# Eight slabs of each gated layer computed by seven block products instead of eight, in a two-block transformer kernel

## The chip, the cores and the metric
One core of one Trainium2 chip (trn2). The metric is the device time of one execution in microseconds; the kernel of before has a median of 1393.8 us over 3 runs (1392.55 to 1393.85).

## The reference, cut to what matters
The program computes two transformer blocks on 512 tokens of width 1024, in float32. Each ends in a gated feed-forward layer of width 2816 (22 tiles of 128). Only these two layers and the down projections behind them are touched:

```
# first block
h = h + (silu(hn @ w_gate) * (hn @ w_up)) @ w_down        # 1024 -> 2 x 2816 -> 1024
# second block: u = h @ w_up, a convolution of 3 taps over the tokens, then
# silu(u[:, :2816]) * u[:, 2816:], then @ w_down
```
Everything is computed to float32's precision. A float32 product on TensorE is made of three fp32r products, with each operand split in a high and a low part: hi x hi + hi x lo + lo x hi.

## The kernel before
**Data and slabs.** Activations lie feature-major, `[128, k, 512]`: feature within a tile of 128, tile k of 8, token. Weights are streamed from HBM as 111 slabs of 1 MB, `[128, 8, 256]`, in one order (`STREAM`): each holds 256 output columns for all 1024 inputs. In the gated layers slab t holds 128 columns of the gate and the 128 matching ones of the value, and its two results go to two banks of PSUM, a pair; `lin` has four banks, so two pairs. Slab g uses buffers `raw[g % 2]`, `whi[g % 2]`, `wlo[g % 2]`, and both layers start at an even g.

**A slab's way.** SyncE loads it into `raw` when GpSimd has finished with the slab two before (`wlo_ready`). ScalarE makes the high part `whi` in one instruction (L419, L746, L851), when TensorE has finished with the slab two before. GpSimd makes the low part `wlo = raw - whi` in four quarters (`low_quarter`, L392). TensorE waits for `wlo_ready` and for its pair of banks (`pair_free`) and issues for each of 2 x 8 tiles the three products of `three` (L1397 to L1401), 48 of 512 columns (`slab_fm`, L1403; `project`, L1439). In four slabs ("mix_tm") the roles are turned: the tokens are stationary and the weights move, 96 products of 256 columns each.

**The gated layers.** After each slab of the first layer VectorE multiplies both banks with the tokens' `rstd` (L1215, L1216) and frees the pair, makes one tile of the modulation that the second block needs (`ada_tile`, L1206; 48 tiles in all, the first 22 here), and multiplies gate and value (L1223). ScalarE makes the next high part first, then the silu (L748), then the high part of the product, `fh` (L750). VectorE makes the low part `fl` (L1225). In the second layer ScalarE evacuates both banks with scale and bias (L847), makes the next high part (L851), the silu (L853) and `fh` (L855); VectorE adds four shifted taps (L1362 to L1368), gates (L1372) and makes `fl` (L1375). Both layers are loops of 11 turns over two slabs. `fh` and `fl` take 44 KB per partition each, in an 88 KB region whose other tenants are dead by then.

**Down** (L1788) is 12 slabs: for each of 4 pairs of output tiles 8, 8 and 6 tiles of the 22 are contracted. Its first three slabs wait until as many low parts exist as they read (8, 16, 22). While it runs VectorE makes 18 more modulation tiles and the residual.

**Order.** Every engine's instructions are executed in the order in which they are written; only semaphores couple the engines. Large tensors start at multiples of 128 bytes (`rstd` is rounded to that, small tensors to 64, which puts `con` at 64 modulo 128).

## Time and profile before
| what | value |
|---|---|
| median of 3 runs | 1393.8 us |
| the profiled execution's own time | 1392.41 us |
| its span in the profile | 1390.6 us |
| instructions | 17280 |
| first gated layer, TensorE | about 481 to 720 us |
| second gated layer, TensorE | about 1025 to 1267 us |

A time in the profile counts from the start of the span. PE is TensorE's products, PEld its weight loads, DVE VectorE, ACT ScalarE, POOL GpSimd. "x4" after a row means that four instructions were merged, and its duration is that of all. A product's duration is longer than the distance to the next one, since products are pipelined; distances between starts give the pace.

### The profile page before, as it was taken

To read this page: it belongs to the slowest core of one execution; us is meant where nothing else is said; L and a number is where in the kernel's file an instruction comes from. 1 tells how busy PE (TensorE), PEld (TensorE's weight loads), DVE (VectorE), ACT (ScalarE), POOL (GpSimd) and SP (SyncE) were. 2 spreads that over 40 slices of the span, in tenths; PEclk is the share of its full clock that TensorE was granted. 3 is DMA by queue.
4 is the path that set the end of the run, shared out by engine and by line. 5 is a ranking of instruction groups with operands and counts; after the bars stand their busy time and mean duration, and the time that the engine had idled before them with its cause. 6 is when DMAs were issued, how large, how long until landed. Compare 5 with 4: busy or idle time off the path is not lost.

```text
span 1390.6 us, 17280 instructions
## 1 busy us (share of the span) xinstructions
PE 1358.4 (98%) x6530; PEld 1091.2 (78%) x6530; DVE 663.4 (48%) x978; ACT 623.4 (45%) x867; POOL 613.5 (44%) x448
## 2 busy tenths in 40 slices
PE   9999999999999999999999999988999999999999
PEld 7877955888876888888888887854878888888887
DVE  5434948355452553444343317588255455554111
ACT  5555228553364443444432123688244545554211
POOL 3444320474430455556554544312326555555453
PEclk9999999999999999999999999999999999999999
DMA  7223211152210244444446433200312222323422
GB/s 269 91 90 102 79 48 74 61 182 91 91 66 27 91 152 141 144 153 151 136 140 268 169 134 106 92 31 31 122 61 90 90 95 96 110 90 136 181 92 91
DMA packets 29215, 155.23 MB, mean 112 GB/s; under 512 B 3056, under 2 KB 4464, under 8 KB 14960
## 3 DMA queue, kind: packets, MB, share of 16 engines
q1 hardware_dynamic: 29168, 154.57, 31.2%
q8 instruction: 34, 0.56, 0.2%
q14 instruction: 13, 0.11, 0.0%
HBM read 152.46 MB, written 2.10 MB: 111 GB/s over the span
## 4 chain that ended last, share of the span: by engine, by line
issue 39%; PE 30%; POOL 26%; DVE 4%; DMA 1%; POOLq 0%; SPq 0%; ACT 0%
POOL wlo L392 26%; PE lin L1399 10%; PE lin L1401 10%; PE lin L1400 10%; DVE small L1044 1%; DVE expd L1055 1%; DMA raw<-w_slabs 1%; PE lin L1616 0%; DVE win L1276 0%; DVE small L1048 0%; POOLq L401 0%; DVE xl L923 0%; PE c_act L1455 0%; PE att L1470 0%; PE att L1464 0%
## 5 line engine op out<-in xcount | busy, mean ns | idle before, releaser
L392 POOL TENSOR_TENSOR wlo<-raw,whi 128x512 fp32r<-128x512 f32 x444 | 613.3, 1413 | 761.7 <-ACT whi L419 501.3
L1399 PE MATMUL lin<-xh,whi 128*128 128x512 f32 x1072 | 420.3, 392 | 4.1 <-POOL wlo L392 3.6
L1401 PE MATMUL lin<-xh,wlo 128*128 128x512 f32 x1072 | 417.3, 389 | 0.0
L1400 PE MATMUL lin<-xl,whi 128*128 128x512 f32 x1072 | 417.2, 389 | 0.0
L419 ACT ACTIVATE whi<-raw 128x2048 fp32r<-128x2048 f32 x66 | 126.6, 1919 | 260.3 <-PE lin L1401 254.9
L1399 PEld LDWEIGHTS lin<-xh,whi 128*128 128x128 f32 x1072 | 201.2, 188 | 52.4 <-issue 7.6
L1401 PEld LDWEIGHTS lin<-xh,wlo 128*128 128x128 f32 x1072 | 201.2, 188 | 42.1
L1400 PEld LDWEIGHTS lin<-xl,whi 128*128 128x128 f32 x1072 | 201.3, 188 | 41.6 <-issue 0.5
L1399 PE MATMUL lin<-fh,whi 128*128 128x512 f32 x352 | 137.0, 389 | 0.0
L1401 PE MATMUL lin<-fh,wlo 128*128 128x512 f32 x352 | 136.9, 389 | 0.0
L1400 PE MATMUL lin<-fl,whi 128*128 128x512 f32 x352 | 136.9, 389 | 0.0
L1206 DVE CUSTOM_DVE_ANT_0 adar<-adar,c_act 128x1024 f32<-128x1024 f32 x48 | 57.8, 1214 | 41.4 <-DMA adar<-ada 41.1
L1401 PEld LDWEIGHTS lin<-fh,wlo 128*128 128x128 f32 x352 | 66.1, 188 | 13.9
L1400 PEld LDWEIGHTS lin<-fl,whi 128*128 128x128 f32 x352 | 66.1, 188 | 13.8
L1399 PEld LDWEIGHTS lin<-fh,whi 128*128 128x128 f32 x352 | 66.1, 188 | 13.7 <-issue 0.3
L1138 DVE SCALAR_TENSOR_TENSOR h<-lin,mod,h 128x512 f32<-128x512 f32 x16 | 11.9, 750 | 118.5 <-PE lin L1401 118.5
L1362 DVE SCALAR_TENSOR_TENSOR tmp<-lin,convp,tmp 128x511 f32<-128x511 f32 x44 | 31.2, 750 | 68.3 <-ACT tmp L847 68.3
L746 ACT ACTIVATE whi<-raw 128x2048 fp32r<-128x2048 f32 x22 | 42.2, 1920 | 40.5 <-PE lin L1401 40.4
L1136 DVE TENSOR_TENSOR h<-lin,h 128x512 f32<-128x512 f32 x24 | 16.4, 691 | 84.2 <-PE lin L1401 84.1
L1215 DVE TENSOR_TENSOR tmp<-lin,rstd 128x512 f32<-128x512 f32 x22 | 15.2, 692 | 82.3 <-PE lin L1401 82.1
L1399 PE MATMUL lin<-xah,whi 128*128 128x512 f32 x128 | 50.7, 396 | 0.0
L1401 PE MATMUL lin<-xah,wlo 128*128 128x512 f32 x128 | 49.9, 390 | 0.0
(334 smaller groups left out, 1923.8 us busy)
## 6 DMA issues: line engine op xcount, KB each, us to landing
raw<-w_slabs SPq DMA_DIRECT2D x111, 1024.0 KB, 4.8
adar<-ada SPq DMA_DIRECT2D x48, 512.0 KB, 5.6
decay<-decay SPq DMA_DIRECT2D x4, 512.0 KB, 7.8
h<-x_t SPq DMA_DIRECT2D x3, 512.0 KB, 6.5
out_t<-h SPq DMA_DIRECT2D x3, 512.0 KB, 8.1
rope<-rope SPq DMA_DIRECT2D x2, 512.0 KB, 7.3
memx<-mem_t SPq DMA_DIRECT2D x1, 1024.0 KB, 5.7
adar<-c_row SPq DMA_DIRECT2D x2, 512.0 KB, 6.2
```

The source lines that it names most:

```text
L392: return nc.gpsimd.tensor_tensor(wlo[s][:, ks, :], raw[s][:, ks, :], f(whi[s][:, ks, :]), ALU.subtract)
L419: nc.scalar.activation(whi[g % 2][:, :, :], raw[g % 2][:, :, :], ACT.Copy).then_inc(whi_ready, 1)
L746: nc.scalar.activation(whi[s][:, :, :], raw[s][:, :, :], ACT.Copy).then_inc(whi_ready, 1)
L1044: last = nc.vector.tensor_reduce(ring(j, "max")[:, e:e + 1], att[n % 4][:, 0:width(j)], AX.X, ALU.max, negate=True)
L1055: nc.vector.tensor_scalar(row, row, ring(j - 1, "inverse")[:, e:e + 1], None, ALU.mult).then_inc(a["norm"], 1)
L1136: ins = nc.vector.tensor_tensor(h[:, k, :], b[:, :], h[:, k, :], ALU.add)
L1206: return nc.vector.tensor_tensor_reduce(adar[s][:, :], adar[s][:, :], c_act[:, :], 1.0, 0.0, ALU.mult, ALU.add, total).then_inc(ada["acc"], 1)
L1215: nc.vector.tensor_tensor(tmp[s][:, :], lin[2 * p][:, :], rstd[:, :], ALU.mult).then_inc(ffn["g"], 1)
L1362: nc.vector.scalar_tensor_tensor(t[:, 1:T], b[:, 0:T - 1], convp[s][:, 4 * j:4 * j + 1], t[:, 1:T], ALU.mult, ALU.add).then_inc(ffn2["tap" ...
L1399: nc.tensor.matmul(out, whi_, xhi_, start=first, stop=False)
L1400: nc.tensor.matmul(out, whi_, xlo_, start=False, stop=False)
L1401: return nc.tensor.matmul(out, wlo_, xhi_, start=False, stop=last)
```

## The change
Slabs 5, 7, ... 19 (`SEVENS`) of each gated layer are computed in another way. The 1024 inputs are taken as even and odd tiles (two blocks of 4 tiles), the 256 columns of the slab as gate and value, the 512 tokens as two halves of 256. So the slab's product is one of 2 x 2 block matrices, which the exact scheme of Strassen and Winograd gives with seven block products and fifteen block sums. The sums:
- of the moving operand (activations), four `[128, 4, 256]` sums, once for each layer: `moving_sums` on VectorE, 3, 2, 2 and 2 instructions, two before slab 0's evacuation and one each after slabs 0 and 1; their high parts by ScalarE (`MOVING_HI`), their low parts `tl` by VectorE after slabs 2 and 3 (`moving_low`), both in the 88 KB region.
- of the stationary operand (weights), four `[128, 4, 128]` sums for each slab on VectorE, `weight_sums`.
- of the products: a copy of the first by ScalarE (`seven_copy`) and seven instructions of 256 columns on VectorE, `combine`, in `lin` and two further banks, `att[0:2]`.

TensorE issues for each of the seven phases 4 x 3 products of 256 columns. The seven stationary units are split one by one, high part by ScalarE and low part by GpSimd, 512 elements each. They take the place of `whi[1]` and `wlo[1]` and the upper part of the region; `raw[1]` is read directly. In each product one operand lies at 64 modulo 128 bytes and the other at 0: the sums of the activations, a11, a12 and s4 at 64, the plain activations, s1, s2, s3 and a22 at 0.

As the region is thus taken, the gated product is kept whole (`gated`), and is split only when slab 19 is through: parts 0 to 4 after slab 20, 5 to 21 after slab 21 on ScalarE. VectorE makes low parts 0 to 4 after slab 20; in the first layer 5 to 9 after slab 21 and 10 to 21 ahead of the modulation tiles, in the second 5 to 21 after slab 21. Down reads these. The loops of ScalarE, VectorE and TensorE over both layers are unrolled; the copies of the convolution's parameters (L1356) and of the modulation sum (L1220) are gone. In the second layer ScalarE's order for each slab is: the seven splits where slab t + 2 is a seven slab, the evacuation of slab t, the copy for slab t + 1, otherwise the plain high part, the silu. VectorE's there: `seven_ended`, four taps, combinations 1 and 2 of slab t + 1, the gating, combinations 3 and 4.

```diff
+SEVENS = range(5, 20, 2)
+LAST_SEVEN = SEVENS[-1]
+PHASES = ("a11", "s2", "s1", "s3", "a12", "s4", "a22")
+MADE = ("a11", "a12", "s1", "s3", "s2", "a22", "s4")
+GATED = {"ffn": 0, "ffn2": 1}
+MOVING_HI = {0: (0, 1), 1: (2,), 2: (3,)}
+GATED_HIGH = {20: range(0, 5), 21: range(5, FT)}
...
-        at[0] = -(-at[0] // 128) * 128
+        at[0] += (P - at[0]) % (2 * P)
...
+        gated = rg_sb("gated", [P, FT, T], 0)
+        gated_lo = rg_sb("gated_lo", [P, FT, T], 0, F32R)
+        gated_hi = rg_sb("gated_hi", [P, FT, T], 44, F32R)
+        sevens = region + 44 * 1024 + 64
+        th = sb("th", [P, 4, TT, COLS], F32R, offset=sevens)
+        tl = sb("tl", [P, 4, TT, COLS], F32R, offset=sevens + 16 * 1024)
+        t_sum = sb("t_sum", [P, 4, TT, COLS], offset=sevens + 16 * 1024)
...
+        for i, u in enumerate(("s1", "s2", "s3", "a22")):
+            unit_hi[u], unit_lo[u] = (sb(f"{u}_{n}", [P, TT, P], F32R, offset=w + 8192 + 2048 * i)
+                                      for n, w in (("hi", whi_at), ("lo", wlo_at)))
+        for i, u in enumerate(("a11", "a12", "s4")):
+            unit_hi[u], unit_lo[u] = (sb(f"{u}_{n}", [P, TT, P], F32R, offset=sevens + (32 + 6 * j + 2 * i) * 1024)
+                                      for j, n in enumerate(("hi", "lo")))
+        for u in ("s1", "s2", "s3"):
+            unit_sum[u] = sb(f"{u}_sum", [P, TT, P], offset=wlo_at + 8192 + 2048 * (int(u[1]) - 1))
+        unit_sum["s4"] = sb("s4_sum", [P, TT, P], offset=sevens + 42 * 1024)
...
+                    made = 0
+                    for u in MADE:
+                        if u == "s4":
+                            pool_e.wait_ge(whi_ready, g + 1)
+                        else:
+                            made += 1
+                            pool_e.wait_ge(seven["hi"], c["hi"] + made)
+                        if u in ("s1", "s2"):
+                            pool_e.wait_ge(seven["sum"], c["sum"] + (2 if u == "s1" else 4))
+                        full = PLAIN[u] if u in PLAIN else unit_sum[u][:, :, :]
+                        ins = nc.gpsimd.tensor_tensor(unit_lo[u][:, :, :], full, f(unit_hi[u][:, :, :]), ALU.subtract)
+                        if u == "a22":
+                            ins.then_inc(wlo_ready, 1)
+                        else:
+                            ins.then_inc(seven["lo"], 1)
...
+            def seven_hi(name, t):
+                g, n = SLAB0[name] + t, SEVENS.index(t)
+                c, before = seven_at(name, n), seven_at(name, n - 1)
+                act.wait_ge(raw_in[1], 16 * (g // 2 + 1))
+                for u in MADE:
+                    if u in PLAIN:
+                        if n and u != "a22":
+                            act.wait_ge(seven["mm"], before["mm"] + PHASES.index(u) + 1)
+                        else:
+                            act.wait_ge(slab_done, g - 1)
+                    else:
+                        act.wait_ge(seven["sum"], c["sum"] + int(u[1]))
+                    full = PLAIN[u] if u in PLAIN else unit_sum[u][:, :, :]
+                    ins = nc.scalar.activation(unit_hi[u][:, :, :], full, ACT.Copy)
+                    if u == "s4":
+                        ins.then_inc(whi_ready, 1)
+                    else:
+                        ins.then_inc(seven["hi"], 1)
+            def seven_copy(name, t, dst):
+                c = seven_at(name, SEVENS.index(t))
+                act.wait_ge(glu["y"], GATED[name] * FT + t - 1)
+                act.wait_ge(seven["mm"], c["mm"] + 1)
+                nc.scalar.activation(dst[:, 0:COLS], lin[2 * ((PAIR0[name] + t) % 2)][:, 0:COLS], ACT.Copy
+                                     ).then_inc(seven["copy"], 1)
...
+            def gated_high(name, t):
+                act.wait_ge(slab_done, SLAB0[name] + LAST_SEVEN + 1)
+                act.wait_ge(glu["y"], GATED[name] * FT + t + 1)
+                nc.scalar.activation(gated_hi[:, t, :], gated[:, t, :], ACT.Copy).then_inc(glu["hi"], 1)
...
+            for t in range(FT):
+                s, g = t % 2, SLAB0["ffn"] + t
+                if t + 2 in SEVENS:
+                    seven_hi("ffn", t + 2)
+                else:
+                    act.wait_ge(slab_done, g + 1)
+                    make_hi(g + 2)
+                if t + 1 in SEVENS:
+                    seven_copy("ffn", t + 1, tmp[1])
+                act.wait_ge(glu["first"], t + 1)
+                nc.scalar.activation(tmp[s][:, :], tmp[s][:, :], ACT.Silu).then_inc(glu["act"], 1)
+                for j in MOVING_HI.get(t, ()):
+                    moving_hi("ffn", j)
+                for j in GATED_HIGH.get(t, ()):
+                    gated_high("ffn", j)
...
+            def weight_sums(name, t, which):
+                n = SEVENS.index(t)
+                c, before, g = seven_at(name, n), seven_at(name, n - 1), SLAB0[name] + t
+                s1, s2, s3, s4 = (unit_sum[f"s{i}"][:, :, :] for i in range(1, 5))
+                ops = {1: (s1, A21, A22, ALU.add), 2: (s2, s1, A11, ALU.subtract), 3: (s3, A21, A11, ALU.subtract),
+                       4: (s4, A12, s2, ALU.subtract)}
+                for i in which:
+                    if i == 1:
+                        dve.wait_ge(raw_in[1], 16 * (g // 2 + 1))
+                    if n:
+                        dve.wait_ge(seven["mm"], before["mm"] + PHASES.index(f"s{i}") + 1)
+                    else:
+                        dve.wait_ge(slab_done, g - 1)
+                    if i in (2, 4):
+                        dve.wait_ge(seven["sum"], c["sum"] + i - 1)
+                    dst, a, b, op = ops[i]
+                    nc.vector.tensor_tensor(dst, a, b, op).then_inc(seven["sum"], 1)
...
+            def combine(name, t, which, s1):
+                c, p = seven_at(name, SEVENS.index(t)), 2 * ((PAIR0[name] + t) % 2)
+                low, high = slice(0, COLS), slice(COLS, T)
+                (ba, bd), (bb, bc) = lin[p:p + 2], att[0:2]
+                u2, u4 = tmp[3][:, low], tmp[3][:, high]
+                for i in which:
+                    if i == 1:
+                        dve.wait_ge(seven["copy"], c["copy"] + 1)
+                        dve.wait_ge(seven["mm"], c["mm"] + 2)
+                        ins = nc.vector.tensor_tensor(u2, bb[:, low], s1[:, low], ALU.add)
+                    if i == 2:
+                        dve.wait_ge(seven["mm"], c["mm"] + 3)
+                        dve.wait_ge(seven["add"], c["add"] + 1)
+                        ins = nc.vector.tensor_tensor(u4, u2, bd[:, low], ALU.subtract)
+                    if i in (3, 4):
+                        dve.wait_ge(seven["mm"], c["mm"] + 4)
+                        dve.wait_ge(seven["add"], c["add"] + 2)
+                        ins = nc.vector.tensor_tensor(bd[:, high] if i == 3 else u2, bc[:, low], u4 if i == 3 else u2, ALU.add)
+                    if i == 5:
+                        dve.wait_ge(seven["mm"], c["mm"] + 5)
+                        ins = nc.vector.tensor_tensor(ba[:, low], ba[:, high], s1[:, low], ALU.add)
+                    if i == 6:
+                        dve.wait_ge(seven["mm"], c["mm"] + 6)
+                        dve.wait_ge(seven["add"], c["add"] + 5)
+                        ins = nc.vector.tensor_tensor(ba[:, high], bb[:, high], u4, ALU.add)
+                    if i == 7:
+                        dve.wait_ge(slab_done, SLAB0[name] + t + 1)
+                        ins = nc.vector.tensor_tensor(bd[:, low], bc[:, high], u2, ALU.add)
+                    ins.then_inc(seven["add"], 1)
...
+            def seven_ended(name, t, s1):
+                if t + 2 in SEVENS:
+                    weight_sums(name, t + 2, (1, 2, 3))
+                combine(name, t, (5, 6), s1)
+                if t + 2 in SEVENS:
+                    weight_sums(name, t + 2, (4,))
+                combine(name, t, (7,), s1)
+                dve.wait_ge(seven["add"], seven_at(name, SEVENS.index(t))["add"] + 7)
...
+            for j in range(2):
+                moving_sums("ffn", norms["ffn"], j)
+            for t in range(FT):
+                s, p = t % 2, (PAIR0["ffn"] + t) % 2
+                if t in SEVENS:
+                    seven_ended("ffn", t, tmp[1])
+                dve.wait_ge(slab_done, SLAB0["ffn"] + t + 1)
+                nc.vector.tensor_tensor(tmp[s][:, :], lin[2 * p][:, :], rstd[:, :], ALU.mult).then_inc(glu["first"], 1)
+                nc.vector.tensor_tensor(tmp[2 + s][:, :], lin[2 * p + 1][:, :], rstd[:, :], ALU.mult).then_inc(pair_free, 1)
+                dve.wait_ge(ada_in[s], 16 * (t // 2 + 1))
+                ada_tile(s, mod[:, t:t + 1])
+                if t + 1 in SEVENS:
+                    combine("ffn", t + 1, (1, 2), tmp[1])
+                if t + 2 == SEVENS[0]:
+                    weight_sums("ffn", t + 2, (1, 2, 3, 4))
+                dve.wait_ge(glu["act"], t + 1)
+                dve.wait_ge(pair_free, PAIR0["ffn"] + t + 3)
+                nc.vector.tensor_tensor(gated[:, t, :], tmp[s][:, :], tmp[2 + s][:, :], ALU.mult).then_inc(glu["y"], 1)
+                if t + 1 in SEVENS:
+                    combine("ffn", t + 1, (3, 4), tmp[1])
+                if t < 2:
+                    moving_sums("ffn", norms["ffn"], t + 2)
+                elif t < 4:
+                    for j in (2 * t - 4, 2 * t - 3):
+                        moving_low("ffn", j)
+                for j in GATED_HIGH[20] if t == 20 else range(5, 10) if t == 21 else ():
+                    gated_low("ffn", j)
...
+                for j in range(10 + 6 * batch, 16 + 6 * batch):
+                    gated_low("ffn", j)
+            lows_beside_down(0)
+            lows_beside_down(1)
...
+                for j in GATED_HIGH[20] if t == 20 else range(5, FT) if t == 21 else ():
+                    gated_low("ffn2", j)
...
+                operands = dict(a11=(ba, plain(0, 0)), s2=(bb, summed(1)), s1=(bd, summed(0)), s3=(bc, summed(2)),
+                                a12=(ba, plain(1, 0)), s4=(bb, plain(1, 1)), a22=(bc, summed(3)))
+                for i, u in enumerate(PHASES):
+                    if i == 0:
+                        pe.wait_ge(pair_free, p + 1)
+                    if n == 0 and i == 1:
+                        pe.wait_ge(seven["add"], c["add"])
+                    if u == "a22":
+                        pe.wait_ge(wlo_ready, g + 1)
+                    else:
+                        pe.wait_ge(seven["lo"], c["lo"] + [m for m in MADE if m != "a22"].index(u) + 1)
+                    if u == "a12":
+                        pe.wait_ge(seven["copy"], c["copy"] + 1)
+                    if u == "s4":
+                        pe.wait_ge(seven["add"], c["add"] + 1)
+                    if u == "a22":
+                        pe.wait_ge(seven["add"], c["add"] + 4)
+                    bank, x = operands[u]
+                    e = int(u in ("a12", "s4", "a22"))
+                    for k in range(TT):
+                        mm = three(bank[:, COLS * e:COLS * (e + 1)], unit_hi[u][:, k, :], unit_lo[u][:, k, :], x[k][0], x[k][1],
+                                   k == 0, k == TT - 1)
+                    if u == "a22":
+                        mm.then_inc(slab_done, 1)
+                    else:
+                        mm.then_inc(seven["mm"], 1)
...
-                            pe.wait_ge(parts["lo"], ks[-1] + 1)
+                            pe.wait_ge(glu["lo"], base + ks[-1] + 1)
```

## Rows read from the trace of the kernel before

**Rows 1.** the page, part 1: busy time, share of the span, instructions of each engine
```profile
PE 1358.4 (98%) x6530; PEld 1091.2 (78%) x6530; DVE 663.4 (48%) x978; ACT 623.4 (45%) x867; POOL 613.5 (44%) x448
```

**Rows 2.** windows view, two slabs of the first gated layer, per engine
```profile
core 0: us, PE busy (x) PEld busy (x) DVE busy (x) ACT busy (x) POOL busy (x), PEclk, DMA share, GB/s
604.00:625.80 21.80, 21.80 (x98) 18.05 (x97) 8.86 (x14) 8.86 (x9) 11.92 (x9) 1.00 0.42 144
```

**Rows 3.** timeline of TensorE in the first gated layer: start, duration, instruction
```profile
520.20 0.39 PE L1399 MATMUL lin<-xh,whi 128*128 128x512 f32 x1
...
522.92 0.39 PE L1399 MATMUL lin<-xh,whi 128*128 128x512 f32 x1
```

**Rows 4.** timeline of TensorE in the token-major projections
```profile
149.90 0.28 PE L1399 MATMUL lin<-whi,xh 128*128 128x256 f32 x1
...
152.90 0.28 PE L1400 MATMUL lin<-wlo,xh 128*128 128x256 f32 x1
```

**Rows 5.** timeline of TensorE at the start of the first down projection
```profile
719.89 0.39 PE L1401 MATMUL lin<-xh,wlo 128*128 128x512 f32 x1
720.12 0.39 PE L1399 MATMUL lin<-fh,whi 128*128 128x512 f32 x1
```

**Rows 6.** timeline of GpSimd in the first down projection
```profile
744.13 5.02 POOL L392 TENSOR_TENSOR wlo<-raw,whi 128x512 fp32r<-128x512 f32 x4 [5.84 <-ACT whi L419]
```

**Rows 7.** timelines of VectorE, ScalarE and GpSimd, one slab of the first gated layer
```profile
611.52 0.69 DVE L1215 TENSOR_TENSOR tmp<-lin,rstd 128x512 f32<-128x512 f32 x1 [2.73 <-PE lin L1401]
612.73 1.21 DVE L1206 CUSTOM_DVE_ANT_0 adar<-adar,c_act 128x1024 f32<-128x1024 f32 x1
...
614.20 1.16 DVE L1223 TENSOR_TENSOR tmp<-tmp,tmp 128x512 f32<-128x512 f32 x1
616.38 0.69 DVE L1225 TENSOR_TENSOR fl<-tmp,fh 128x512 f32 x1 [1.02 <-ACT fh L750]
...
613.34 0.61 ACT L748 ACTIVATE tmp<-tmp 128x512 f32<-128x512 f32 x1
...
613.52 5.95 POOL L392 TENSOR_TENSOR wlo<-raw,whi 128x512 fp32r<-128x512 f32 x4 [3.58 <-ACT whi L746]
```

**Rows 8.** instructions grouped by line and form
```profile
L976 DVE TENSOR_TENSOR tmp<-tmp,rope 128x512 f32<-128x512 f32 x8 | 5.4, 681 | 0.0
L930 DVE TENSOR_TENSOR wlo<-raw,whi 128x512 fp32r<-128x512 f32 x3 | 2.0, 683 | 0.0
L1034 DVE TENSOR_TENSOR weight<-att,decay 128x256 f32<-128x256 f32 x8 | 3.0, 411 | 0.0
L1512 PE MATMUL att<-squares,con 128*128 128x512 f32 x8 | 3.8, 592 | 0.0
```

**Rows 9.** timeline of VectorE at the end of the residual before the first gated layer
```profile
483.88 1.77 DVE L881 TENSOR_TENSOR rstd<-rstd,tmp 128x512 f32<-128x512 f32 x1
```

**Rows 10.** timelines of ScalarE, VectorE and GpSimd, one slab of the second gated layer
```profile
1201.77 1.45 ACT L847 ACTIVATE tmp<-lin,convp 128x512 f32<-128x512 f32 x2 [2.42 <-PE lin L1401]
1203.11 1.91 ACT L851 ACTIVATE whi<-raw 128x2048 fp32r<-128x2048 f32 x1
...
1203.92 0.74 DVE L1365 SCALAR_TENSOR_TENSOR tmp<-lin,convp,tmp 128x511 f32<-128x511 f32 x1
...
1205.10 5.93 POOL L392 TENSOR_TENSOR wlo<-raw,whi 128x512 fp32r<-128x512 f32 x4 [3.67 <-ACT whi L851]
```

**Rows 11.** timeline of VectorE, first two slabs of the first gated layer
```profile
493.39 0.69 DVE L1215 TENSOR_TENSOR tmp<-lin,rstd 128x512 f32<-128x512 f32 x1 [0.23 <-DVE rstd L1202]
...
502.72 0.69 DVE L1215 TENSOR_TENSOR tmp<-lin,rstd 128x512 f32<-128x512 f32 x1 [2.72 <-PE lin L1401]
```

**Rows 12.** windows view around the softmax of the cross attention, columns as in rows 2
```profile
411.30:414.70 3.40, 2.43 (x14) 1.75 (x15) 3.33 (x7) 1.87 (x7) 3.40 (x3) 1.00 0.00 0
414.76:418.16 3.40, 3.40 (x6) 1.33 (x5) 0.91 (x4) 3.25 (x6) 0.24 (x1) 0.50 0.56 164
```

**Rows 13.** timeline of TensorE, f32 products from squares and con
```profile
127.20 1.88 PE L1512 MATMUL att<-squares,con 128*128 128x512 f32 x4
```

232 lines of the change are left out of this document (141 added, 91 removed).

## The prediction, made before the changed kernel ran
> **What bounds the kernel now.** The page comes first. TensorE is busy 98% of the span, VectorE, ScalarE and GpSimd under half [rows 1]. The windows view of one pair of slabs in the first gated layer shows the same: TensorE without a gap, the others busy for 9 to 12 of 21.8 us [rows 2]. So time is won only by giving TensorE less to do, and is lost wherever it is made to wait. The timeline then gives its pace. Twelve products of 512 columns take 520.20 to 522.92, 226.7 ns each [rows 3]; 25 products of 256 columns take 149.90 to 152.90, 120.0 ns each [rows 4]. Columns at 2.4 GHz are 213.3 and 106.7 ns, so about 13.3 ns per product come on top at either width. The boundary from the first gated layer to its down projection is also seamless: the next product starts 0.23 us after the last [rows 5].
>
> **1. TensorE's own work.** A plain slab is 48 products of 512 columns: 48 x 0.2267 = 10.88 us. A seven-product slab is 7 x 4 x 3 = 84 products of 256: 84 x 0.120 = 10.08 us. Arithmetic falls by an eighth, but there are more products, each with its 13.3 ns, so only 0.80 us is won. Sixteen slabs: **-12.8 us**. This is the whole gain; everything else can only take from it.
> The Trainium skill (TensorE: Matmul & The Clock Gate, Back-to-back issue gap) puts the fixed part of a warm product at 2.5 ns. By it the slabs would take 10.36 and 9.17 us and the gain would be 19.0 us. No fp32r row here shows so small a part, so the sum doesn't use it.
>
> **2. The price of a shared access.** The weights' low parts (GpSimd) meet VectorE instructions with two SBUF sources. GpSimd's four quarters take 5.02 us undisturbed [rows 6], 1.26 each, and 5.95 in a gated slab, where VectorE runs two such instructions [rows 7]: 0.46 more each. On VectorE's side one of 512 elements takes 0.68 alone [rows 8], but 1.77 when it must let a quarter finish [rows 9]. Side by side they thus alternate at 1.26 + 0.46 = 1.72 us a turn. The changed kernel adds such instructions: weight sums, moving sums and their low parts, and it moves the gated low parts together.
> The Trainium skill (SBUF — State Buffer, two separate sides) states the rule behind this and it speaks against the change: VectorE with two SBUF inputs and GpSimd lock each other out for a whole instruction. The trace agrees in kind; an entire lockout would add 0.68 rather than 0.46.
>
> **3. Steady state, per pair (even slab, seven slab, 20.96 us).** GpSimd: 4 quarters and 7 unit subtractions of the same 512 elements, 11 x 1.26 + 6 crossings x 0.46 = 16.6 us. ScalarE in the second layer, its fuller one: 1.92 for the plain weights, 7 x 0.61, a copy near 0.4, 4 x 0.73, 2 x 0.61: 10.7. VectorE there: 8 taps of 0.74, 2 gatings and 4 weight sums of 0.68 to 1.72, 7 combinations of 0.41 [rows 8]: 12.9 to 19.1. All fit. The order matters at one place: the low parts of the even slab that follows a seven slab. Count from the end of the even slab before. First layer: ScalarE's high part at once, 1.92; GpSimd 5.02 with one or two crossings, ready at 7.5; needed at 10.08. No wait. Second layer: ScalarE first evacuates the pair, 1.45 [rows 10], then the new copy, 0.4, then 1.92: 3.8. GpSimd needs 5.02 and crosses the gating and two or three weight sums for the slab after, 1.4: ready at 10.2 to 10.9, wanted at 10.08. Seven slabs wait about 0.35 us: **+2.5** (bounds 0 and 7 x 0.9 = 6). The products of the seven slab wait for nothing: first copy at 2.3 for the fifth product at 5.8, combinations 3 and 4 at 6.7 for the seventh at 8.6.
>
> **4. The front of each layer.** Before the first slab's evacuation VectorE makes the first two moving sums, 5 chained instructions of 1024 elements, 1.22 us each going by 411 and 683 ns for 256 and 512 [rows 8], 2.3 if GpSimd alternates. In the first layer they stand behind the reciprocal: first evacuation at 493.4 + 6.1 = 499.5 to 504, where it was 493.39; TensorE needs its banks when slab 1 ends, 502.7 [rows 11]. I take 1 us (0 to 2.5). In the second layer nothing is in the way. At slab 3 VectorE has, besides the evacuation, four weight sums, a gating that waits until ScalarE has split all seven units, and two moving lows of 1024; slab 5's second product waits for these at 12.3 us, and they end at 10 to 16. I take 1.5 and 1. Together **+3.5** (0 to 9).
>
> **5. The boundary to down.** Before, the gated high and low parts were made slab by slab, and down started with all but the last. Now their place is occupied by the seven scheme until slab 19, ScalarE makes parts 0 to 4 after slab 20 and 5 to 21 only after the silu of slab 21. Down's first slab waits for low parts 0 to 7. So parts 5 to 7 are entirely behind the end of slab 21. First layer, VectorE: two evacuations 1.37, modulation tile 1.29, gating 0.68, three lows 2.04: 5.4 us at least (ScalarE: 1.92 + 0.61 + 3 x 0.63, then a low, 5.1). GpSimd is subtracting the next weights from 2.0 on, so gating and lows alternate with its four quarters: 3.3 + 0.65, then three turns of 1.72: 9.2. Second layer: the evacuation costs 3.7, ScalarE reaches the silu at 4.05 behind 1.45 + 1.92, then gating and three lows: 6.8 at least, 10.7 alternating from 3.5. Rows of one such instruction after another beside GpSimd are nearest to alternation [rows 9], so I take 9.2 + 10.7: **+19.9** (12.2 to 19.9). Nothing covers this: TensorE has no other work there, and all later work shifts with it.
>
> **6. The clock.** Before 414.7 TensorE worked 2.43 of 3.40 us; in the 3.40 us that follow its clock is at half, 1.2 GHz [rows 12]. A pause of 9 us should do no less. Each such stretch costs up to 1.7 us if work falls in it: **+2.5** for two (0 to 3.4).
>
> **7. Without effect.** Unrolling removes ScalarE's table loads in the loops, and VectorE's convp copies and ada_sum copies go. They stood beside TensorE's work, which had no gap there, so they are worth nothing by themselves. SyncE's loads keep their conditions: the weights of an odd slab are requested once unit a22 of the odd slab before has been subtracted, about 4 us before that slab starts on TensorE, and their first new reader, ScalarE's first unit, comes 3 us after its start. In down the modulation tiles start after twelve more lows, but the weights' own condition comes later still. Moving rstd and tmp by 256 bytes keeps their position modulo 128.
>
> **Sum.** -12.8 + 2.5 + 3.5 + 19.9 + 2.5 = **+15.6 us**. The profiled execution took 1392.4 (span 1390.6), giving 1408.0; the median, 1393.8, is 1.4 higher, so 1409. All lower bounds: -12.8 + 12.2 = -0.6, or 1393; all upper: +25.5, or 1419.
>
> **Rivals.** (a) *Placement, faster.* Every fp32r operand of before lies at 0 modulo 128 bytes; in the changed kernel each small product has one operand at 0 and one at 64. The f32 products that have con at 64 show almost nothing on top: four take 1.88 us where one takes 0.59 [rows 8, 13], so 0.43 apart for two passes of 0.213. If the fixed part falls from 13.3 to 3 ns for these 1344 products, that is another -13.8. The even slabs of the second layer would then wait 0.85 longer (+6), so with the boundary at 19.9 the result stays slower, 1401. It turns below 1391 only where VectorE also wins the access at once (12.2, front and clock near 0): 1393.8 - 26.6 + 12.2 + 6 = 1385. Against: f32 products with both operands at 0 look no different. Chance of faster 0.12. (b) *No contention at the boundary.* VectorE gets in between the quarters each time, pauses of 5.4 and 6.8, the clock hardly falls: -0.6 to +2, 1393 to 1396. The single low part in rows 7 takes only 0.69 beside GpSimd, but it comes after a pause of VectorE. Chance 0.10. (c) *GpSimd becomes the bound.* It is at 16.6 of 21; if its unit subtractions over strided weights cost 2 us rather than 1.45, every odd slab starts late, 16 x 0.8 more: 1422. The same size takes 1.49 where VectorE crosses it [rows 7]; chance 0.08, inside slower. (d) *Boundary hidden*, gain 12.8 whole, 1381: excluded by the program order on ScalarE, except by a misreading; it is in the 0.12.
>
> **How the numbers follow.** My case and its neighbours between +3 and +25 hold 0.70, (c) 0.08, (b) 0.10, faster 0.12. A measurement of this kernel tells about 0.2% from nothing, 2.8 us. The range leaves out most of faster and part of (c): 1392 to 1419.
>
> **What would show it.** Starts of the 256-column products 120 ns apart confirm step 1; 109 would be rival (a). TensorE idle behind GpSimd's wlo before even slabs of the second layer only: step 3. One gap of about 9 and one near 11 us before down's first products, released by VectorE's gated_lo: step 5; under 7 both, rival (b). The granted clock at half right after each: step 6. A total under 1391 would prove the sum wrong.

## The result, and the profile after

| what | before | after |
|---|---|---|
| median, us | 1393.17 (4 runs, 1392.32 to 1393.85) | 1409.85 (4 runs, 1406.78 to 1411.55) |
| profiled execution, us | 1392.41 | 1409.14 |
| its span, us | 1390.6 | 1407.4 |

The change makes the kernel slower: ratio 1.0118, 95% interval 1.0098 to 1.0137. Of the page of after, busy time, share and instructions of each engine; these answer to [rows 1]:

```profile
PE 1346.3 (96%) x7106; PEld 1107.5 (79%) x7106; DVE 808.3 (57%) x1136; ACT 611.5 (43%) x945; POOL 695.4 (49%) x496
```
TensorE is busy for 12.1 us less and the span is 16.8 us longer: the work did shrink, and 28.9 us of idle TensorE came in.

**Where TensorE waits.** The timeline of TensorE in after, in order of time: before slab 2 of the first layer, at the boundary to down (answers to [rows 5]), before slab 5's second block product and before an even slab of the second layer, and at the second boundary:

```profile
503.75 0.39 PE L1638 MATMUL lin<-xh,wlo 128*128 128x512 f32 x1
506.26 0.47 PE L1636 MATMUL lin<-xh,whi 128*128 128x512 f32 x1 [2.12 <-DVE tmp L1432]
...
717.34 0.39 PE L1638 MATMUL lin<-xh,wlo 128*128 128x512 f32 x1
726.82 0.76 PE L1636 MATMUL lin<-gated_hi,whi 128*128 128x512 f32 x1 [9.09 <-DVE gated_lo L1409]
...
1092.19 0.39 PE L1636 MATMUL att<-th,s_hi 128*128 128x256 f32 x1 [1.55 <-DVE tl L1352]
...
1122.09 0.50 PE L1636 MATMUL lin<-xh,whi 128*128 128x512 f32 x1 [0.48 <-POOL wlo L430]
...
1271.48 0.39 PE L1638 MATMUL lin<-xh,wlo 128*128 128x512 f32 x1
1282.23 0.76 PE L1636 MATMUL lin<-gated_hi,whi 128*128 128x512 f32 x1 [10.36 <-DVE gated_lo L1409]
```
The bracket is the idle time and what ended it. Measured by starts (717.34 to 726.82 is 9.48, less the pace of 0.227), the two big pauses are 9.25 and 10.52 us and end with VectorE's last gated low part.

**Why VectorE is late there.** Timelines of VectorE and of GpSimd in after, from the end of the first layer's last slab:

```profile
717.76 0.69 DVE L1431 TENSOR_TENSOR tmp<-lin,rstd 128x512 f32<-128x512 f32 x1 [0.65 <-PE lin L1638]
...
718.97 1.21 DVE L1324 CUSTOM_DVE_ANT_0 adar<-adar,c_act 128x1024 f32<-128x1024 f32 x1
...
720.31 1.34 DVE L1441 TENSOR_TENSOR gated<-tmp,tmp 128x512 f32<-128x512 f32 x1
721.58 7.50 DVE L1409 TENSOR_TENSOR gated_lo<-gated,gated_hi 128x512 fp32r<-128x512 f32 x7
...
719.83 6.29 POOL L430 TENSOR_TENSOR wlo<-raw,whi 128x512 fp32r<-128x512 f32 x4 [4.48 <-ACT whi L488]
```
The gating takes 1.34 instead of 0.68, and seven low parts 7.50, while GpSimd's four quarters take 6.29 instead of 5.02 [rows 6]. TensorE resumes at 726.8, when GpSimd has just ended at 726.1.

**The clock.** Windows view of after, around the first boundary, columns as in [rows 2]:

```profile
705.00:717.70 12.70, 12.70 (x57) 10.20 (x55) 10.10 (x10) 5.04 (x7) 6.39 (x4) 1.00 0.41 137
...
719.80:730.00 10.20, 3.18 (x8) 2.54 (x9) 10.08 (x12) 10.18 (x19) 6.29 (x4) 0.50 0.41 140
```
Some 2.2 us into the pause the granted clock falls to a half, 1.2 GHz, for 10.24 us; the first eight products of down run in that stretch. At the second boundary the fall comes 4.4 us into the pause and lasts as long.

**The pace of the small products.** Timeline of TensorE in after, the starts of the seven block products of slab 11 in the order of `PHASES` (a11, s2, s1, s3, a12, s4, a22), and of the slab behind it:

```profile
624.07 0.28 PE L1636 MATMUL lin<-xh,a_hi 128*128 128x256 f32 x1
...
625.49 0.28 PE L1636 MATMUL att<-th,s_hi 128*128 128x256 f32 x1
...
626.90 0.28 PE L1636 MATMUL lin<-th,s_hi 128*128 128x256 f32 x1
...
628.32 0.28 PE L1636 MATMUL att<-th,s_hi 128*128 128x256 f32 x1
...
629.73 0.28 PE L1636 MATMUL lin<-xh,a_hi 128*128 128x256 f32 x1
...
631.10 0.28 PE L1636 MATMUL att<-xh,s_hi 128*128 128x256 f32 x1
...
632.46 0.28 PE L1636 MATMUL att<-th,a_hi 128*128 128x256 f32 x1
...
633.82 0.39 PE L1636 MATMUL lin<-xh,whi 128*128 128x512 f32 x1
```
Twelve products each: the first four take 1.41 to 1.42 us (117.5 to 118 ns a product), the last three 1.36 or 1.37 (113.3 to 114.2). The whole slab of 84 takes 9.75 us, 116.1 ns a product, and so do the others but slab 5 once their waits are taken off; that is neither the 120.0 of [rows 4] nor rival (a)'s 109.

### The profile page after: what moved, and what is told of

Its sections match the earlier page's. It is cut to its first block, busy times and chain, and to the rows that moved or that the text cites. A ratio compares the mean times of both kernels' runs of the same rounds, so it can differ in the third digit from the quotient of the medians.

```text
span 1407.4 us, 18385 instructions
## 1 busy us (share of the span) xinstructions
PE 1346.3 (96%) x7106; PEld 1107.5 (79%) x7106; DVE 808.3 (57%) x1136; ACT 611.5 (43%) x945; POOL 695.4 (49%) x496
## 4 chain that ended last, share of the span: by engine, by line
PE 47%; issue 24%; POOL 18%; DVE 8%; ACT 2%; DMA 0%; SPq 0%; POOLq 0%; DVEq 0%; ACTq 0%
POOL wlo L430 17%; PE lin L1636 14%; PE lin L1638 13%; PE lin L1637 13%; DVE small L1162 1%; PE att L1636 1%; DVE expd L1173 1%; PE att L1638 1%; PE att L1637 1%; ACT whi L488 1%; PE lin L2049 1%; DVE s_sum L1373 1%; ACT tmp L963 1%; DVE tl L1352 0%; DMA raw<-w_slabs 0%
## 5 line engine op out<-in xcount | busy, mean ns | idle before, releaser
L430 POOL TENSOR_TENSOR wlo<-raw,whi 128x512 fp32r<-128x512 f32 x380 | 526.9, 1418 | 691.8 <-ACT whi L488 660.7
L1636 PE MATMUL lin<-xh,whi 128*128 128x512 f32 x816 | 320.8, 393 | 9.9 <-POOL wlo L430 6.4
L1637 PE MATMUL lin<-xl,whi 128*128 128x512 f32 x816 | 317.8, 389 | 0.0
L1638 PE MATMUL lin<-xh,wlo 128*128 128x512 f32 x816 | 317.7, 389 | 0.0
L1636 PE MATMUL lin<-gated_hi,whi 128*128 128x512 f32 x352 | 138.7, 394 | 19.4 <-DVE gated_lo L1409 19.4
L1637 PE MATMUL lin<-gated_lo,whi 128*128 128x512 f32 x352 | 138.2, 393 | 0.0
L1638 PE MATMUL lin<-gated_hi,wlo 128*128 128x512 f32 x352 | 138.1, 392 | 0.0
L1636 PEld LDWEIGHTS lin<-gated_hi,whi 128*128 128x128 f32 x352 | 67.0, 190 | 34.1 <-issue 20.2
L466 POOL TENSOR_TENSOR s_lo<-s_sum,s_hi 128x512 fp32r<-128x512 f32 x64 | 91.8, 1455 | 1.5 <-DVE s_sum L1373 1.5
L466 POOL TENSOR_TENSOR a_lo<-raw,a_hi 128x512 fp32r<-128x512 f32 x48 | 79.0, 1660 | 3.3 <-ACT a_hi L513 3.3
```

The lines of the kernel that those rows point to most:

```text
L430: return nc.gpsimd.tensor_tensor(wlo[s][:, ks, :], raw[s][:, ks, :], f(whi[s][:, ks, :]), ALU.subtract)
L466: ins = nc.gpsimd.tensor_tensor(unit_lo[u][:, :, :], full, f(unit_hi[u][:, :, :]), ALU.subtract)
L1636: nc.tensor.matmul(out, whi_, xhi_, start=first, stop=False)
L1637: nc.tensor.matmul(out, whi_, xlo_, start=False, stop=False)
L1638: return nc.tensor.matmul(out, wlo_, xhi_, start=False, stop=last)
```

## The experiments

The twelve kernels fall in four groups, each timed beside the kernel before on the same chip. Code is cut at `...`. The kernel before had medians of 1393.75, 1392.42, 1391.9 and 1393.77 there, so a difference of a us or two across groups means nothing.

**First group (before 1393.75).** *1. The deferral alone.* All slabs plain, no sums, but the gated product is split as late as in the change and the loops stay unrolled.

```diff
-SEVENS = range(5, 20, 2)
-LAST_SEVEN = SEVENS[-1]
+SEVENS = ()
+LAST_SEVEN = 19
...
```


> The changed kernel with no seven-product slab at all: every slab plain, but the gated parts still split only after slabs 20 and 21, and the loops still unrolled. Theory (the boundary waits are the cost, and they come from the deferral alone): TensorE waits 9 and 10.5 us before the two down projections, about 3.7 us of half clock after them, no waits inside the layers, some 1.8 us gained in the second layer by the unrolling; 1393.2 + 9.1 + 10.4 + 3.7 - 1.8 = 1415 us. Rival (the seven-product machinery, its sums and its contention, is the cost): about the time of the kernel before, 1391 to 1396.

1414.10 us, ratio 1.0143 (1.0127 to 1.0158). The waits view of this kernel, TensorE (us in total, times, longest):

```profile
PE lin L1616 <- DVE gated_lo L1405: 19.5, 2, 10.4
```
All of the loss is the deferral. The seven products with everything they drag along are worth only about 4 us (1414.10 - 1409.85). In the second layer, moreover, TensorE has no pause at all between slabs, which bears on the unrolling below.

*2. All operands at 0 modulo 128 bytes.*

```diff
-        sevens = region + 44 * 1024 + 64
+        sevens = region + 44 * 1024 + 128
```


> The changed kernel with its new operands at 0 modulo 128 bytes instead of 64; the operations are the same. In the changed kernel's trace the products of the seven slabs start 113 to 118 ns apart, against 120 in the token-major projections. Theory (the distance comes from the two operands' places): they go back to 120 ns, 1344 x 2.7 ns = 3.6 us more, 1413.5. Rival (it comes from something else in these products, the placing does nothing): 117 ns and 1409.9 as before.

1413.28 us, ratio 1.0145 (1.0131 to 1.0159). Its timeline at the same block products:

```profile
628.09 0.28 PE L1636 MATMUL att<-th,s_hi 128*128 128x256 f32 x1
...
629.53 0.28 PE L1636 MATMUL lin<-xh,a_hi 128*128 128x256 f32 x1
...
630.96 0.28 PE L1636 MATMUL att<-xh,s_hi 128*128 128x256 f32 x1
```
1.44 and 1.43 us for twelve, 120.0 and 119.2 ns; a whole slab takes 10.03 us (119.4 ns a product) instead of 9.75. The placing is worth 16 x 0.28 = 4.5 us, of which 6 x 0.25 = 1.5 are given back, since the even slabs of the second layer wait 0.64 with it and 0.39 without. The medians are 3.4 us apart.

*3. Eight parts early.* ScalarE and VectorE split parts 0 to 7 after slab 20, all that down's first slab reads.

```diff
-GATED_HIGH = {20: range(0, 5), 21: range(5, FT)}
+GATED_HIGH = {20: range(0, 8), 21: range(8, FT)}
...
```


> The changed kernel with gated parts 0 to 7, not 0 to 4, split after slab 20, so that down's first slab waits for nothing that follows slab 21. Theory: the waits of 9.1 and 10.4 us shrink to about 2 and 3.5 us, in which VectorE ends the low parts, and the half clock after them mostly goes: 1409.9 - 14 - 3.5 = 1392. Rival (the wait only moves to down's second slab, which needs parts up to 15): the two waits reappear before it and the time stays over 1402.

1393.15 us, ratio 1.0003 (0.9992 to 1.0014). The two waits shrink from 19.8 to 1.49 + 2.76 us, and instead of two half-clock stretches of 10.24 at the boundaries there is one of 3.4. They didn't reappear in down's second slab.

*4. No GpSimd beside the low parts.* Parts 5 to 7 stay late, but after slab 21 ScalarE makes them ahead of the next weights' high part, so that GpSimd has nothing to subtract meanwhile.

```diff
-                else:
+                elif t < 21:
...
+                    if t == 21 and j == 8:
+                        make_hi(g + 2)
...
```


> The changed kernel with one change of order on ScalarE after slab 21 of each layer: silu and gated high parts 5 to 7 first, the high part of down's second slab of weights after them. GpSimd is then idle while VectorE makes low parts 5 to 7. Theory (VectorE's low parts lose 1 us each to GpSimd's quarters): TensorE's waits fall from 9.1 to about 5.5 and from 10.4 to about 7, 1402.5. Rival (VectorE is paced by ScalarE's high parts or its own work, not by GpSimd): the waits change by under 1 us each, 1409.

1403.83 us, ratio 1.0078 (1.0063 to 1.0094). Timelines of VectorE and GpSimd of this kernel at the boundary:

```profile
719.03 0.69 DVE L1445 TENSOR_TENSOR gated<-tmp,tmp 128x512 f32<-128x512 f32 x1
719.64 1.89 DVE L1413 TENSOR_TENSOR gated_lo<-gated,gated_hi 128x512 fp32r<-128x512 f32 x3
721.96 3.04 DVE L1413 TENSOR_TENSOR gated_lo<-gated,gated_hi 128x512 fp32r<-128x512 f32 x2 [0.44 <-ACT gated_hi L536]
...
721.48 4.68 POOL L430 TENSOR_TENSOR wlo<-raw,whi 128x512 fp32r<-128x512 f32 x3 [7.20 <-ACT whi L488]
```
The gating takes 0.69 and three low parts 1.89, and the moment GpSimd starts at 721.48 two low parts take 3.04. The pauses are 5.18 and 6.50, against 9.25 and 10.52: 4.1 and 4.0 us less. Some 0.2 of each come from an earlier silu and gating, the rest, 3.8 us a boundary, is what the shared access costs: 0.65 in the gating and 3.1 in the three low parts. That is the alternation of step 2, seen with and without its partner. The time fell by only 6 us, since the clock gave nothing back: its half-clock stretches are shorter (3.4 and 6.8 us) but lie wholly or mostly in down's work, whose first slab takes 12.6 and 13.5 us here, 12.5 and 12.9 in after and 10.88 in before.

**Second group (before 1392.42).** *5. The front.* In the first layer two moving sums each after slabs 0 and 1 and none before slab 0's evacuation; in both layers the low parts 2 and 3 ahead of slab 3's gating.

```diff
-            for j in range(2):
-                moving_sums("ffn", norms["ffn"], j)
...
-                    moving_sums("ffn", norms["ffn"], t + 2)
+                    for j in (2 * t, 2 * t + 1):
+                        moving_sums("ffn", norms["ffn"], j)
...
+                if t == 3:
+                    for j in (2, 3):
+                        moving_low("ffn2", j)
...
```


> The changed kernel with VectorE's sums placed otherwise: in the first layer the moving sums 0 and 1 after slab 0's evacuation and gating, 2 and 3 after slab 1's; in both layers the moving lows 2 and 3 ahead of slab 3's gating, which waits for ScalarE. Theory (the waits of 2.3 us before slab 2 of the first layer and of 2.35 and 1.7 us inside slab 5 of each layer are VectorE's order alone): all three go or fall under 0.5 us, 1409.9 - 6 = 1404. Rival (VectorE simply has too much to do by slab 5, wherever it stands): the wait before slab 2 goes, those inside slab 5 stay or grow, 1407 to 1409.

1403.97 us, ratio 1.0079 (1.0064 to 1.0095). Both waits of the first layer are gone, that of the second fell from 1.72 to 1.10 with 0.84 at the next even slab, and the boundary is untouched (9.27 and 10.53). The waits that went come to 2.3 + 2.4 + 0.6 - 0.8 = 4.4 us; the medians differ by 5.9, beside each kernel's own before by 5.1.

*6. Everything at once, with the order of test 4.* All eight seven slabs; eight parts early; TensorE waits tile by tile in down; the next slab's high part behind the gated ones to part 11; the copy behind the plain high part; the front of test 5.

> The changed kernel, still with eight seven-product slabs in each layer, with four mends together: gated parts 0 to 7 split after slab 20 and down waiting tile by tile instead of for eight at once; the high part of down's second slab of weights after gated high part 11; the sums placed as in the run on the front; in the second layer the copy of the first product after the plain high part. Theory (the waits are separate and additive, nothing else bounds): no wait over 0.5 us in either layer or at the boundaries, so 1393.2 - 1.8 (unrolling) - 16 x 1.0 = about 1376 to 1379. Rival (contention on VectorE and GpSimd brings new waits in their place): over 1385.

1387.52 us, ratio 0.9957 (0.9943 to 0.9970): faster than before, but far from the expected. Timelines of ScalarE, GpSimd and TensorE of this kernel in down's first slabs:

```profile
716.09 1.90 ACT L488 ACTIVATE whi<-raw 128x2048 fp32r<-128x2048 f32 x1
717.90 5.30 ACT L536 ACTIVATE gated_hi<-gated 128x512 fp32r<-128x512 f32 x10
...
718.07 6.36 POOL L430 TENSOR_TENSOR wlo<-raw,whi 128x512 fp32r<-128x512 f32 x4 [8.79 <-ACT whi L488]
...
724.49 0.50 PE L1644 MATMUL lin<-gated_hi,whi 128*128 128x512 f32 x1 [1.96 <-POOL wlo L430]
```
The trick that helped in test 4 hurts here. The weights' high part, 4.3 us later behind slab 21 than in test 11 (5.7 in the second layer), is now what down's second slab waits for: 2.12 us here and 4.72 at 1266.6, with a half-clock stretch of 6.8 us around its end.

*7. Seven seven-slabs instead of eight.* Slab 19 becomes plain, so the region comes free two slabs earlier and the gated parts are spread over slabs 18 to 21. The copy, the tile-wise wait and the front as in test 6, the high part in its natural place.

```diff
-SEVENS = range(5, 20, 2)
+SEVENS = range(5, 18, 2)
...
-GATED_HIGH = {20: range(0, 5), 21: range(5, FT)}
+GATED_HIGH = {18: range(0, 4), 19: range(4, 9), 20: range(9, 15), 21: range(15, FT)}
...
```


> As the run before it in the list, but with seven-product slabs 5 to 17 only, seven in each layer, and the gated parts split during slabs 18 to 21, so that all but the last seven are ready when down begins. Theory: 14 x 1.0 + 1.8 us less than the kernel before and no waits, 1377 to 1380, about the same as with eight and mended boundaries. Rival (with 22 parts to split in four slabs VectorE is late): waits over 1 us before down, over 1382.

1380.12 us, ratio 0.9901 (0.9886 to 0.9916). Both boundaries are without a wait.

*8. The kernel before with its split weights 64 bytes further on.* If 64 modulo 128 helps small products, it might help all. The parameters and constants that lie behind the weights move along.

```diff
+        at[0] += 64
         whi = [sb(f"whi{i}", [P, KT, COLS], F32R) for i in range(2)]
```


> The kernel before, with one line: the weights' high and low parts (whi, wlo) start 64 bytes later, so that every slab product has its weights at 64 modulo 128 bytes and its activations at 0. No operation changes. Theory (two operands of an fp32r product at the same place modulo 128 bytes cost about 3 ns a product, as the run with aligned operands showed for the small ones): the distance of 512-column products falls from 226.7 to about 223, over 4000 products, 12 to 16 us, 1379. Rival (the effect is of the 256-column products alone, or of th and tl): 1393 to 1394.

1419.97 us, ratio 1.0188 (1.0170 to 1.0205): the opposite. The timeline of TensorE of this kernel, products of 512 columns:

```profile
619.76 0.39 PE L1400 MATMUL lin<-xh,whi 128*128 128x512 f32 x1
...
622.56 0.39 PE L1400 MATMUL lin<-xh,whi 128*128 128x512 f32 x1
```
Twelve products in 2.80 us, 233.3 ns each, where [rows 3] has 226.7. Those of 256 columns went the other way, from 120.0 to 117.8 in the token-major projections. The expectation took a gain at one width for a gain at every width.

**Third group (before 1391.9).** *9. The copy later.* In the second layer alone ScalarE makes the plain high part ahead of the copy.

```diff
-                if t + 1 in SEVENS:
-                    seven_copy("ffn2", t + 1, tmp[2])
                 if t + 2 not in SEVENS:
                     make_hi(g + 2)
+                if t + 1 in SEVENS:
+                    seven_copy("ffn2", t + 1, tmp[2])
```


> In the second gated layer ScalarE makes the next plain high part before the copy instead of after it; nothing else changes. If the wait of the even slab after a seven slab (0.64 us, six times) comes from the copy's 0.4 us ahead of the high part, it falls to about 0.25 to 0.36 and the time by 1 to 3 us, to about 1407.5, with the two waits before down unchanged. Rival, the copy is too late then for the fifth block product and the seven slabs themselves begin to wait: no change or slower, 1410 to 1413.

1408.12 us, ratio 1.0122 (1.0105 to 1.0139). The six waits are 0.37 instead of 0.64, 1.6 us together. The time is 1.7 us under after, 0.5 beside each kernel's own before, and the profiled spans differ by 0.8. The difference alone is within the scatter of the runs; the shorter waits are not.

*10. The tile-wise wait.* Test 3, and TensorE waits in down for one low part at a time.

```diff
-                            pe.wait_ge(glu["lo"], base + ks[-1] + 1)
...
+                                if m == 0 and j == 0:
+                                    pe.wait_ge(glu["lo"], base + k + 1)
```


> As the version with eight parts split after slab 20 (1393.2), and TensorE waits for the gated low parts tile by tile in down. If only the first tiles' wait counted, waits of 1.5 and 2.8 us vanish: 1389 to 1390. If the low parts come more slowly than TensorE takes them (1.72 us a turn against 6 products of 0.227, 1.36 us), the wait returns a few tiles on, at most a third smaller: 1392.

1385.89 us, ratio 0.9959 (0.9945 to 0.9973), better than either case. Of 4.25 us of waits 0.47 are left (at 1284.2), and the half-clock stretch behind the second wait went too, which the expectation forgot: up to 1.7 us; and the kernel before was 1.85 us faster here than beside test 3. 1393.15 - 3.8 - 1.7 - 1.85 is 1385.8; that it fits to 0.1 is luck, as the five times of this kernel spread over 2.8 us.

*11. All eight, with the natural order.* Test 6 without its late high part.

> All eight seven slabs; eight parts split after slab 20, TensorE waits tile by tile in down, the next slab's high part stays ahead of the gated ones on ScalarE, the copy after the plain high part, the moving sums later. If the waits inside down of the version that made the next high part late (2.1 and 4.7 us, both on GpSimd's weights) came from that lateness, they go: 1393.2 - 5.9 (front) - 1.5 (copy) - 3.5 (by tile) = 1382, down to 1379. Rival, the thirteen or fourteen lows that are still to be made beside GpSimd's quarters are late in any order, since they alternate at 1.72 us a turn: they wait at some later tile and it stays at 1386 to 1388.

1376.43 us, ratio 0.9896 (0.9880 to 0.9913): **15.5 us under the kernel before beside it, and some 33 under the change as it was made.** The windows view of this kernel over the whole first layer, and the waits view of TensorE, the lines that concern the gated layers:

```profile
481.00:720.00 239.00, 239.00 (x1381) 210.81 (x1380) 188.14 (x227) 94.34 (x132) 175.56 (x116) 1.00 0.45 148
```
```profile
PE lin L1640 <- POOL wlo L430: 8.1, 13, 2.1
...
PE att L1640 <- DVE tl L1352: 0.9, 1, 0.9
```
TensorE has no idle moment in 239 us, the boundary to down among them. What is left in the second layer is 1.11 by starts at slab 5, six waits of 0.36 (part of the first line, whose rest lies outside the layers) and 0.47 in down. It is 2.6 us under the lowest that was expected. Since 6 and 11 differ in one order only, the late high part alone cost 11 us. Between 7 and 11 lie 3.7 us in the medians (3.2 beside their own kernel before), but their intervals overlap; by the traces the eighth seven slab in each layer takes 2 x 1.1 us from TensorE and adds waits of 0.5 behind it and 0.5 in down, so that it pays about 1.2 us once the boundary is hidden.

**Fourth group (before 1393.77).** *12. Everything at 64.* The kernel before with activations, weights and region all at 64 modulo 128 bytes.

```diff
-        at = [-(-nc.sbuf_base // 64) * 64]
+        at = [-(-nc.sbuf_base // 128) * 128 + 64]
...
-        at[0] = -(-at[0] // 128) * 128
+        at[0] = -(-at[0] // 128) * 128 + 64
```


> The kernel before with every large tensor, the activations as well as the weights, at 64 modulo 128 bytes; nothing else changes. With the weights alone at 64 the products of 512 columns went from 226.7 to 233.3 ns and those of 256 from 120.0 to 118.1, and the time to 1420. If what counts is that the two operands of a product lie differently, both at 64 behave as both at 0: 226.7 and 120.0 ns, 1392 to 1394. If it is an operand at 64 in itself that changes the pace, products of 512 stay at 233 ns or above: 1415 or more.

1392.71 us, ratio 0.9996 (0.9986 to 1.0007). Its timeline, products of 512 columns:

```profile
619.73 0.39 PE L1400 MATMUL lin<-xl,whi 128*128 128x512 f32 x1
...
622.45 0.39 PE L1400 MATMUL lin<-xl,whi 128*128 128x512 f32 x1
```
2.72 us for twelve, 226.7 ns, and those of 256 columns are back at 120.0. Both operands at 64 change nothing; what counts, as far as it was tried, is whether the two operands of a product lie alike.

## Why the prediction was right, step by step

The forecast was 1409.0, the result 1409.85. The boundary, which is the big term, and the sign of all the others held. The nearness is luck all the same: by the trace TensorE had 7 us less work than forecast and 8 us more of waits and half clock, and the two cancel. Its sum, set beside the trace of after (each row is how much longer TensorE's slabs or pauses are than in before):

| step | predicted | in the trace |
|---|---|---|
| 1. TensorE's work | -12.8 | -17.8 |
| unrolled loops | 0 | -1.8 |
| 3. even slabs of the second layer | +2.5 | +4.5 |
| 4. front | +3.5 | +7.1 |
| 5. boundaries | +19.9 | +19.8 |
| 6. clock behind the boundaries | +2.5 | +3.7 |
| clock before the layers | none | +1.5 |
| sum | +15.6 | +17.0 (span: +16.8) |

**Step 1** was mis-sized. It took 120.0 ns for every small product; measured are 116.1 and 9.75 us for a slab of 84 with its hand-over, instead of 10.08: 16 x 0.33 = 5.3 us more gain, less 0.3 because the plain slabs between take 10.90 instead of 10.88. Test 2 shows that most of this, 4.5 us, is the placing. So rival (a) had the right cause and a third of its size: 9.4 ns on top of the columns instead of 13.3, not 3. The f32 rows that it leaned on said nothing of fp32r; that their 0.43 us are "two passes" is a reading that no run here tests.
The Trainium skill (TensorE: Matmul & The Clock Gate, Back-to-back issue gap) puts that part at 2.5 ns. The trace of after does not agree: the fastest group here, s4 on x, takes 113.3 against 106.7 of columns, 6.6 ns.

**Unrolling** (in step 7) was costed at nothing, since TensorE "had no gap there". That was read too coarsely. The timeline of TensorE in before, where a new turn of the second layer's loop starts:

```profile
1091.36 0.39 PE L1401 MATMUL lin<-xh,wlo 128*128 128x512 f32 x1
1091.66 0.49 PE L1399 MATMUL lin<-xh,whi 128*128 128x512 f32 x1
1091.99 0.39 PE L1400 MATMUL lin<-xl,whi 128*128 128x512 f32 x1
```
300 and 330 ns instead of 227: 0.18 us a turn, ten times, 1.8 us. In test 1, which has the unrolling and no seven slab, these are gone; the copies of the convolution's parameters went with it, and no run parts the two. The first layer's loop had no such pairs, so why the second had them stays open.

**Step 2**, the price of a shared access, is confirmed by test 4: low parts of 0.63 each alone, 1.5 beside GpSimd, and 3.8 us per boundary for it. The moving sums of 1024 elements show it too. Timelines of VectorE and GpSimd in the version of test 11:

```profile
497.88 2.19 DVE L1344 TENSOR_TENSOR t_sum<-t_sum,xl 128x1024 f32<-128x1024 f32 x1
500.11 1.23 DVE L1346 TENSOR_TENSOR t_sum<-t_sum,xl 128x1024 f32<-128x1024 f32 x1
...
492.52 6.47 POOL L430 TENSOR_TENSOR wlo<-raw,whi 128x512 fp32r<-128x512 f32 x4 [5.87 <-ACT whi L488]
```
GpSimd ends at 498.99; the sum begun before takes 2.19, the next 1.23.
The Trainium skill (SBUF — State Buffer, two separate sides) states that VectorE with two SBUF inputs and GpSimd lock each other out for a whole instruction. The trace agrees in kind: VectorE waits out the quarter that runs, and GpSimd's four take 6.29 instead of 5.02.

**Step 3** held in kind and was mis-sized. Where it expected seven waits of 0.35 there are six of 0.64, released by GpSimd's low part, in the second layer only, each with 0.11 more in the product behind it: a pair takes 21.41 us there and 20.65 in the first layer. The first layer's pairs wait for nothing, and of the seven slabs only slab 5 does (step 4). Test 9 shows that the copy makes 0.27 of the 0.64.

**Step 4** was mis-sized, at all its places. The first evacuation came late enough for 2.3 us at slab 2 where 1 was taken: VectorE's sums met GpSimd, as the timeline of VectorE in after shows:

```profile
500.37 2.20 DVE L1344 TENSOR_TENSOR t_sum<-t_sum,xh 128x1024 f32<-128x1024 f32 x1
502.60 2.19 DVE L1346 TENSOR_TENSOR t_sum<-t_sum,xl 128x1024 f32<-128x1024 f32 x1
504.83 0.69 DVE L1431 TENSOR_TENSOR tmp<-lin,rstd 128x512 f32<-128x512 f32 x1
...
536.53 1.74 DVE L1441 TENSOR_TENSOR gated<-tmp,tmp 128x512 f32<-128x512 f32 x1 [1.22 <-ACT tmp L859]
538.19 4.53 DVE L1352 TENSOR_TENSOR tl<-t_sum,th 128x1024 fp32r<-128x1024 f32 x2
```
The evacuation starts at 504.8 where 499.5 to 504 was given, the step's upper case and a little over. And slab 5's second product waited 2.35 and 1.72 where 1.5 and 1 were taken, because the gating (1.74) and the two moving low parts (4.53) also met it. With a wait of 0.2 before slab 4 of the second layer and the slower products behind each wait this makes 7.1 us, inside the bounds of 0 to 9. Test 5 shows that the order was the cause: with it changed, 4.4 us of the waits go.

**Step 5** held, to 0.1 us in the sum: 9.25 and 10.52 measured against 9.2 and 10.7, with VectorE's gated low part as releaser. Test 1 shows that it stands by itself and test 3 that eight parts early remove it. Rival (b), 5.4 and 6.8, did not come true; it is what test 4 makes of the kernel (5.18 and 6.50), once GpSimd is out of the way.

**Step 6** held in kind. Each pause brings one stretch at half the clock, but of 10.24 us rather than 3.4, and since TensorE idles through most of it, only eight to ten products of 427 instead of 227 ns fall in it: down's first slab takes 12.5 and 12.9 us instead of 10.88, 1.6 + 2.1. The stretch before the layers, at 265.8, lies in a part that the change doesn't touch. The profile of before has none there, that of test 12, which does the same work in the same order as before, has one at 266.7, and that of test 5, whose program is that of after up to there, has none; so it is scatter between runs and not the change's.

**Rival (c)** did not come true. On the page GpSimd's subtraction over strided raw weights does look dearer. Groups by line of GpSimd in after, and two rows of its timeline:

```profile
L430 POOL TENSOR_TENSOR wlo<-raw,whi 128x512 fp32r<-128x512 f32 x380 | 526.9, 1418 | 691.8 <-ACT whi L488 660.7 <-ACT whi L495 31.1
L466 POOL TENSOR_TENSOR a_lo<-raw,a_hi 128x512 fp32r<-128x512 f32 x48 | 79.0, 1660 | 3.3 <-ACT a_hi L513 3.3
...
611.16 3.45 POOL L466 TENSOR_TENSOR a_lo<-raw,a_hi 128x512 fp32r<-128x512 f32 x2
...
619.23 1.30 POOL L466 TENSOR_TENSOR a_lo<-raw,a_hi 128x512 fp32r<-128x512 f32 x1
```
But 1.66 against 1.42 us is a mean over crossings: 39 of the 48 strided ones meet VectorE's sums and take about 1.74, as at 611.16, and the other nine take 1.28 to 1.30, where the undisturbed plain ones take 1.26 to 1.29. The stride costs next to nothing, and a crossing 0.46, as in step 2. At 49% of the span GpSimd never became the bound. **Rival (d)**, the boundary hidden, was excluded rightly for this order of work; tests 7 and 11 show what the order would have to be.

## What to carry to other kernels

An eighth less arithmetic was worth some 18 us of 1390 in TensorE's time where the products shrank to half width, and a handful of instructions whose place in the program was pushed behind the last slab cost more than that: when a buffer's lifetime forces work to be put off, count what the bottleneck engine waits for at the seam first, and split exactly as much as the next stage's first step reads. VectorE's two-source instructions beside GpSimd's should be priced at the alternation, not at their own time. And a fix is valid for its context: making the next weights' high part late won 6 us over the change as made (test 4), and cost 11 in the version where eight parts were early (test 6 against 11).

## What the runs showed of the hardware that was not expected

The position of a product's two operands modulo 128 bytes changes its pace, and the sign depends on the width. With both alike (both at 0 or, test 12, both at 64) fp32r products run at 226.7 ns for 512 columns and 120.0 for 256 in the plain projections. With one at 64 and the other at 0, those of 512 take 233.3 (test 8, 27 us over the kernel), and those of 256 take 117.8 in the token-major projections and 113.3 to 118 in the seven slabs.

Which operand lies where does not explain that last spread: a11 and a12 both have the weights at 64 and x at 0 and take 118 and 114 ns; s3 and a22 both have them at 0 and t at 64 and take 117.5 and 113.3. What the three faster ones (a12, s4, a22) share is that they write the upper half of a bank of PSUM, and that they are the last three of the slab; the four slower ones write the lower half. In test 2, with every operand at 0, the same three take 118.5 to 118.9 and the other four 119.8 to 120.8. No run parts the half of the bank from the order, and the token-major products, which use both halves, show no such difference (117.8 in each, test 8). What lies behind it all is not settled; positions other than 0 and 64 were not tried.
